# First norm and its modulation cut from two halves of the features into four quarters

## The reference, cut to what matters

```python
mod = c @ w_ada[l] + b_ada[l]                       # c: 1 x 1024, w_ada: 1024 x 3072
shift, scale, gate = jnp.split(mod, 3, axis=-1)
h = _rmsnorm(x, norm_g[l]) * (1.0 + scale[:, None, :]) + shift[:, None, :]
proj = h @ w_in[l]                                  # q_a, k_a, v_a, z_a, ... from h
```

## Time and profile before

| | before |
|---|---|
| median of 3 runs | 1303.47 us |
| the profiled execution's own time | 1301.79 us |
| its span in the trace | 1300.0 us |
| PE busy | 1258.9 us (97%) |
| DVE busy | 757.2 us (58%) |
| ACT busy | 585.0 us (45%) |
| POOL busy | 747.1 us (57%) |
| mean granted clock of TensorE | 0.991 |

### The profile page before, as it was taken

One profiled execution on the slowest core, in us unless ns is written; L12 is line 12 of the kernel. 1 busy time (PEld: TensorE's weight loads), 2 busy tenths in 40 slices (PEclk: granted clock), 3 DMA queues, 4 the chain that ended last, 5 costly groups with the idle time before them and its releaser, 6 DMA issues.

```text
span 1300.0 us, 16886 instructions
## 1 busy us (share of the span) xinstructions
PE 1258.9 (97%) x6162; PEld 1047.0 (81%) x6162; DVE 757.2 (58%) x1233; ACT 585.0 (45%) x951; POOL 747.1 (57%) x862
## 2 busy tenths in 40 slices
PE   5989999999999999999999999999999999999997
PEld 4868878878888888887778988888888888888885
DVE  5857788434434367699687427655457616651564
ACT  3366566456655346233456645434333313331341
POOL 2643543433343676676445869534659857885782
PEclk9989999999999999999999999999999999999998
DMA  9421224232334743232214443222313333223221
GB/s 380 168 82 57 81 81 140 96 98 93 110 115 135 242 128 99 81 98 89 61 69 154 131 163 114 81 66 65 93 55 112 100 112 97 97 98 98 97 81 65
DMA packets 41698, 142.46 MB, mean 110 GB/s; under 512 B 4624, under 2 KB 5136, under 8 KB 40464
## 3 DMA queue, kind: packets, MB, share of 16 engines
q1 hardware_dynamic: 41616, 141.39, 32.7%
HBM read 130.88 MB, written 8.39 MB: 107 GB/s over the span
## 4 chain that ended last, share of the span: by engine, by line
PE 70%; DVE 19%; ACT 6%; issue 2%; POOL 1%; DMA 1%; SPq 0%; DVEq 0%; ACTq 0%; POOLq 0%
PE ps L124 69%; DVE tm L137 4%; DVE ac L137 3%; ACT tm L131 3%; DVE tm L134 2%; ACT L131 1%; PE ps L128 1%; DVE x L137 1%; POOL wl L134 1%; DVE ewl L134 1%; DVE spl L134 1%; ACT wh L131 1%; DVE zh L145 1%; DMA x<-xin 1%; DVE ewh L145 1%
## 5 line engine op out<-in xcount | busy, mean ns | idle before, releaser
L134 POOL TENSOR_TENSOR wl<-raw,wh 128x256 fp32r<-128x256 f32 x804 | 690.7, 890 | 496.6 <-ACT wh L131 488.7
L131 ACT ACTIVATE wh<-raw 128x1024 fp32r<-128x1024 f32 x201 | 212.2, 1056 | 319.3 <-PE ps L124 308.2
L124 PE MATMUL ps<-hh,wh 128*128 128x512 f32 x872 | 344.1, 395 | 0.0
L124 PE MATMUL ps<-hh,wl 128*128 128x512 f32 x872 | 340.5, 391 | 0.0
L124 PE MATMUL ps<-hl,wh 128*128 128x512 f32 x872 | 340.3, 390 | 0.0
L124 PEld LDWEIGHTS ps<-hh,wl 128*128 128x128 f32 x872 | 164.1, 188 | 35.1
L124 PEld LDWEIGHTS ps<-hh,wh 128*128 128x128 f32 x872 | 164.2, 188 | 33.3 <-DVE tm L137 0.4
L124 PEld LDWEIGHTS ps<-hl,wh 128*128 128x128 f32 x872 | 164.3, 188 | 33.0
L134 DVE TENSOR_TENSOR tm<-tm,tm 128x512 f32<-128x512 f32 (+3 forms) x110 | 90.7, 829 | 46.5 <-ACT tm L131 43.6
L137 DVE SCALAR_TENSOR_TENSOR tm<-cb,par_sb,tm 128x512 f32<-128x512 f32 x88 | 87.4, 993 | 50.9 <-ACT tm L131 47.5
L131 ACT ACTIVATE tm<-tm 128x512 f32<-128x512 f32 (+3 forms) x109 | 53.8, 530 | 83.8 <-DVE tm L137 67.8
(11 more groups left out here) (305 smaller groups left out, 2281.4 us busy)
## 6 DMA issues: line engine op xcount, KB each, us to landing
raw<-units SPq DMA_DIRECT2D x201, 512.0 KB, 3.5
ada<-units SPq DMA_DIRECT2D x16, 512.0 KB, 14.6
kept<-ge SPq DMA_DIRECT2D x16, 256.0 KB, 2.8
tm<-kept SPq DMA_DIRECT2D x16, 256.0 KB, 3.7
tm<-gate_w SPq DMA_DIRECT2D x12, 256.0 KB, 3.9
x<-xin SPq DMA_DIRECT2D x2, 1024.0 KB, 6.2
x<-xin SPq DMA_DIRECT2D x1, 2048.0 KB, 10.9
out<-x SPq DMA_DIRECT2D x8, 256.0 KB, 2.2
```

Of the source, the lines that this page charges most:

```text
L124: return self.none if self.e is None else self.e.matmul(out, lhs, rhs, start=start, stop=stop, skip_group_check=skip)
L131: return self.none if self.e is None else self.e.activation(out, in_, func, **kw)
L134: return self.none if self.e is None else self.e.tensor_tensor(out, a, b, op)
```

## The change

A unit of w_ada now holds two row blocks (2k and 2k + 1) of 256 columns of scale and 256 of shift, so four units are a quarter of the features (two blocks of h), and there are 4 quarters of 8 steps of 512 columns in place of 2 halves of 8 steps of 1024. `MQ` names the four quarters of `MA` and `MA2`. The sums, gains and shifts are made by quarter, PE starts a step u of the values when the rows of quarter u are there, DVE puts three steps of the next quarter ahead of a quarter's small instructions, one behind its rows and four behind its low rows, and the loads stand in another order. ACT loads the table of the square root after the fourth square. Renamings that follow from it (`s_mod` keys 2 to 4) are left out here.

```diff
-    u = [("ada", a, k) for a in range(2) for k in range(8)]
+    u = [("ada", a, k) for a in range(4) for k in range(4)]
...
-        def ada_sums(a, b, ma):
...
+        def ada_sums(a, b):
+
+            take(b)
+            pe.wait_ge(s_mod, a, 7)
             for f in range(4):
...
+                last = pe.mm(PS[b][:, f:f + 1], MQ[a][:, f * 128:(f + 1) * 128], con_f("one", 1), True, True)
             last.then_inc(*s_modp.up(a))
             bank[b] = (s_modc, (a,))
...
+        ada_sums(0, 0)
         spread("x", 7)
         bank[7] = (s_ht, ("1", 7))
-        ada_sums(0, 0, MA)
-
-        def second_half(u):
+
+        def next_quarter(u):
 
 
             if u == 2:
                 qkz("a", 0, "q", 0)
-                mod_end(1, 6, MA2)
+            if u:
+                ada_sums(u, 6)
+            if u == 2:
                 qkz("a", 0, "k", 0)
...
-                act.wait_ge(s_mod, 0, j - N_ADA + 2)
+                act.wait_ge(s_mod, 1, 2 * (j - N_ADA - 2) + 1)
...
-        act.wait_ge(l_con, 0)
+            if k == 3:
+                act.wait_ge(l_con, 0)
+                act.fn(sm[:, 60:61], con_raw[:, 0:1], ACT.Sqrt)
...
-        def mod_step(a, k, ma):
-            j = 8 * a + k
+        def mod_step(a, k):
+            j, w = 4 * a + k // 2, slice(512 * (k % 2), 512 * (k % 2) + 512)
...
         for k in range(KC):
-            if k == 6:
-                root_inverse("x")
-            mod_step(0, k, MA)
-        mod_pair(0, 0)
...
+            mod_step(0, k)
+        root_inverse("x")
+        for a in range(4):
+
+            steps = list(range(KC)) if a < 3 else []
+            for k in steps[:3]:
+                mod_step(a + 1, k)
+            mod_pair(a, 6 if a else 0)
+            dve.wait_ge(s_gain, "g", a)
+            dve.wait_ge(s_spread, "x")
+            row(2 * a)
+            row(2 * a + 1)
+            for k in steps[3:4]:
+                mod_step(a + 1, k)
+            low_row(2 * a)
+            low_row(2 * a + 1)
+            for k in steps[4:]:
+                mod_step(a + 1, k)
...
-                pool.wait_ge(s_mod, 0, j - N_ADA + 4)
-                if j == N_ADA + 3:
-                    pool.wait_ge(s_ada, 0)
+                pool.wait_ge(s_mod, 1, 2 * (j - N_ADA) + 1)
...
         for j in range(N_ADA):
+            if j == 12:
+                raw(N_ADA + RING)
             sp.dma(ADA[j][:, :], units[j]).then_inc(*l_ada[j].up("ada"))
-            if j in (5, 7, 11, 13):
-                raw(N_ADA + (5, 7, 11, 13).index(j))
+            if j in (3, 4, 7, 9):
+                raw(N_ADA + (3, 4, 7, 9).index(j))
```

More of the change, by code:

```diff
@@ L324, in build @@
     MA2 = at("ma2", [P, U], F32, a1 + 4096)
+    MQ = [t[:, 512 * x:512 * x + 512] for t in (MA, MA2) for x in range(2)]
     o_ada = [h0, h0 + 4096, h0 + 16384, h0 + 20480] + [w0 + 16384 * x + 4096 * y for x in (1, 2) for y in (2, 3)]
@@ L406, in build @@
     s_add, s_root, s_sqrt, s_spread = sig("s_add"), sig("s_root"), sig("s_sqrt"), sig("s_spread")
-    s_conr, s_mk, s_mod, s_ada, s_modp, s_modc, s_gain = (
-        sig(n) for n in ("s_conr", "s_mk", "s_mod", "s_ada", "s_modp", "s_modc", "s_gain"))
+    s_conr, s_mk, s_mod, s_modp, s_modc, s_gain = (
+        sig(n) for n in ("s_conr", "s_mk", "s_mod", "s_modp", "s_modc", "s_gain"))
     s_ht, s_hh, s_hl = sig("s_ht"), sig("s_hh"), sig("s_hl")
@@ L546, in mod_end @@
             bank[b] = (s_modc, (part,))
-        def ada_sums(a, b, ma):
-            pe.wait_ge(s_mod, a, 6)
+        def ada_sums(a, b):
+            take(b)
+            pe.wait_ge(s_mod, a, 7)
             for f in range(4):
-                pe.mm(PS[b][:, f:f + 1], ma[:, f * 128:(f + 1) * 128], con_f("one", 1), f == 0, False, skip=True)
-            pe.wait_ge(l_ada[8 * a + 7], "ada")
-            for f in range(4):
-                last = pe.mm(PS[b][:, f:f + 1], ADA[8 * a + 7][:, f * 128:(f + 1) * 128], pcol("c", 7), False, True,
-                             skip=True)
-            last.then_inc(*s_ada.up(a))
-            pe.wait_ge(s_mod, a, 7)
-            for f in range(4, 8):
-                last = pe.mm(PS[b][:, f:f + 1], ma[:, f * 128:(f + 1) * 128], con_f("one", 1), False, True, skip=True)
+                last = pe.mm(PS[b][:, f:f + 1], MQ[a][:, f * 128:(f + 1) * 128], con_f("one", 1), True, True)
             last.then_inc(*s_modp.up(a))
@@ L1314, in scalar_program @@
         for k in range(KC):
-            act.wait_ge(s_modc, k // 4)
+            act.wait_ge(s_modc, k // 2)
             act.wait_ge(s_ht, "1", k)
             act.fn(HH[:, k, :], TM[(3 + k) % 7][:, :], ACT.Identity, bias=sm[:, k:k + 1]).then_inc(*s_hh.up("1", k))
-            if k == 2:
+            if k == 1:
                 hi(("aq", 0))
+                hi(("ak", 0))
             if k == 3:
-                hi(("ak", 0))
                 refill(("av", 0))
+            if k == 5:
                 refill(("av", 1))
@@ L1852, in mod_pair @@
             dve.wait_ge(s_gain, "one", a)
-            dve.tt(g, g, prow("norm_g", 4, o), ALU.mult).then_inc(*s_gain.up("g", a))
+            dve.tt(g, g, prow("norm_g", 2, o), ALU.mult).then_inc(*s_gain.up("g", a))
         def mod_out(part, b):
             dve.wait_ge(s_modp, part)
-            dve.tt(sm[:, 8 * part:8 * part + 8], PS[b][:, 0:8], prow("b_ada", 8, 8 * part),
+            dve.tt(sm[:, 16:24], PS[b][:, 0:8], prow("b_ada", 8, 16),
                    ALU.add).then_inc(*s_modc.up(part))
@@ L1878, in vector_program @@
         for k in range(KC):
-            if k == 6:
-                root_inverse("x")
-            mod_step(0, k, MA)
-        mod_pair(0, 0)
-        dve.wait_ge(s_gain, "g", 0)
-        dve.wait_ge(s_spread, "x")
-        row(0)
-        row(1)
-        low_row(0)
-        row(2)
-        low_row(1)
-        mod_step(1, 0, MA2)
-        low_row(2)
-        row(3)
-        mod_step(1, 1, MA2)
-        low_row(3)
-        for k in range(2, KC):
-            mod_step(1, k, MA2)
-        mod_pair(1, 6)
-        dve.wait_ge(s_gain, "g", 1)
-        row(4)
-        row(5)
-        for k in range(4, KC):
-            low_row(k)
-            if k < 6:
-                row(k + 2)
+            mod_step(0, k)
[15 more added lines that the diff above has]
+                mod_step(a + 1, k)
         dve.wait_ge(l_cont, 0)
@@ L2062, in gate_add @@
                 dve.wait_ge(l_gate[x], k)
-                key = (2, k) if x else (2, k, "half")
+                key = (4, k) if x else (4, k, "half")
                 if k == 0:
@@ L2666, in sync_program @@
                     sp.dma(KV[:, p0:p1, :], KVT[:, p0:p1, :]).then_inc(*l_kv[x].up(0))
-            raw(j)
+            if j > N_ADA + RING:
+                raw(j)
         for f in range(KC):
@@ L2702, in pack_units @@
         if k == "ada":
-            r, c0 = slice(128 * u[2], 128 * u[2] + 128), 512 * u[1]
-            b = np.concatenate([wada[r, 1024 + c0:1536 + c0], wada[r, c0:512 + c0]], axis=1)
+            c0, b = 256 * u[1], []
+            for k in (2 * u[2], 2 * u[2] + 1):
+                r = slice(128 * k, 128 * k + 128)
+                b += [wada[r, 1024 + c0:1280 + c0], wada[r, c0:256 + c0]]
+            b = np.concatenate(b, axis=1)
         elif k in ("aq", "ak", "az", "bq", "bk", "bz"):
```

29 lines of the change are left out of this document (14 added, 15 removed).

## The result

The changed kernel takes 1311.62 us in the median of six runs (1309.63 to 1312.53), the kernel before 1302.05 beside it (1301.49 to 1304.37): a ratio of 1.0066, with an interval of 1.0056 to 1.0076. It is slower, by some 7 to 10 us; the forecast was 5.5 over the kernel before. (Two executions further down, one of fill_all and one of quarter_sums2, took 2085 us at a granted clock of 0.56 and stand in no median, range or ratio.)

The account below looks back on a forecast made before the run. PE was taken as the bound from 29.39 us. A head start of 3.5 less 8.2 lost in holes, steps and small instructions gave 4.7 later, with the clock +5.5: 1303.47 + 5.5, about 1309, range 1303.5 to 1313.

Parts of the forecast that it names:

- PE as the bound, one to one: From 29.39 us PE works without a hole, so any shift of its memory sums at 63.03 reaches the end whole.
- Head start 3.4 to 3.5: Up to the first matmul: quarter 0's sums and rows finish sooner, first matmul at about 25.9 in place of 29.39.
- The first hole: Behind quarter 1's sums: PE idle from 35.0 to 37.8 us until quarter 1's rows are made.
- The clock: PE behind the holes: at least one fall to half clock expected behind 37.8 us, 1.6 us more.
- The new wait for the memory norm: At PE's memory sums: the norm's chain ends at 67.9, 2 us behind PE, so 63.03 becomes about 67.8, 4.7 later.
- Costed at nothing: Raw 4's load queued ahead of unit 12, and POOL's units at other times with room of 4 us or more: no cost.
- The faster one: Rival, chance 0.12: DVE never waits for the sums and POOL doesn't slow it, so -3.2 us, 1300.3.
- The slow clock's: Rival, chance 0.10: PE's clock falls in each hole and stays down through a value step, +10 to 12 us, 1314.5.
- The middle of the two cases: Half weight between no clock fall and one of 1.6 us, on top of 4.7 us: +5.5 us.

Follow-up runs that it names:

- fill_all: The changed kernel with q and k cut by quarters, each piece straight behind that quarter's sums on PE: 1302.08 us, ratio 1.0000 to the kernel before.
- quarter_sums2: The kernel before with half 0's sums and rows by quarters, and half 1's sums behind q's half and k's blocks 0 and 1: 1303.87 us, ratio 1.0006.
- shift: The kernel before with a chain of eight 128x512 additions on DVE ahead of the first row, delaying the rest: 1309.07 us, ratio 1.0045.
- early_raw: The kernel before with one transfer reordered, weight unit 28 sent ahead of 26 and 27: 1297.63 us, ratio 0.9957.
- fill: The changed kernel with sums straight behind each value step and q's and k's first halves cut into pieces behind them: 1306.20 us, ratio 1.0012 to the kernel before.
- idle_pool: The changed kernel with three of four POOL subtractions of the first six weight units replaced by zero fills: 1306.21 us, ratio 1.0038 to the kernel before.
- fewer_steps: The changed kernel with every second step of DVE's running sums replaced by a one-column instruction: 1308.37 us, ratio 1.0039 to the kernel before.

## Why the prediction was right, point by point

- **PE as the bound, one to one.** One to one is right: shift moved the end by 5.9 for 6.07. PE as the only bound is not. DVE's running sums were level with it at 45.8 us, and the 0.4 us of idling that the prediction names ahead of the earlier trace rows is PE's weight load waiting for them. In shift whatever PE gained went into waits for DVE. That `sph`'s wait comes of the load at 75.83 was right too, and early_raw shows it.
- **Head start 3.4 to 3.5.** 3.66. The sums started at 12.74 (forecast 12.95), the square root ran at 15.45 without a table load, the rows started at 24.02 (24.3). What released them was not what the prediction had: PE's spread was through at 23.4 (24.1), and DVE's three steps and small instructions, 1.39 us beside POOL, lasted to 24.0. That the number came out so near is luck in part. The steps of 512 columns took 0.81 alone and 1.17 beside POOL (0.82 and 1.15): four in 4.70 at 53.32, two in 1.61 at 44.32. Here the Trainium skill's page "VectorE: DVE Perf Modes", section "The TRN2 errata", from which the prediction estimated 0.16 us for cutting a step in two, does not cover the pairs beside POOL, which cost 0.65 more than one step of 1024 (2 x 1.17 less 1.69).
- **The first hole.** Forecast 35.0 to 37.8, measured 34.00 to 37.60. PE's clock rose after 3.4 us of dense matmuls and not after 5.3, so its sums came a microsecond early, and that was lost at once: DVE had the last step of quarter 1 done at 31.4 as costed, but it did not wait from there: three steps of quarter 2 stand ahead of the small instructions in its program and last to 34.5. They would have been hidden behind sums that end at 35.0.
- **The clock.** This is the mis-sized term. One fall of 1.6 us was expected, at half weight. The first hole brought a stretch from 36.0 to 42.8, of which 5.2 us fell on matmuls (2.4 us lost), and the last a second from 63.3 to 66.7 (1.6). Everything from 45 to 60 us came 1.1 to 1.4 later than forecast: sums of quarter 2 at 48.43 (47.0), rows of quarter 3 at 59.83 (58.7). The two falls took 4.0 us where 0.8 was carried.
- **The new wait for the memory norm.** Right on the chain, wrong on the wait. The splits ended at 68.5 (forecast 67.9), but PE, due at 65.9, came at 69.04, late by the 1.1 carried over, the second fall, 1.6, and 0.4 of wider spacing. So 67.8 and 4.7 became 69.04 and 6.0, and the wait for `mpl` that the prediction named as a sign did not show. In fill, which has no fall, the wait shows (0.62). That 5.5 came so near 6.0 at this point is luck in part: PE lost 3.1 us more than forecast, and the 2.0 that it was to be ahead of the splits took up most of that.
- **Costed at nothing.** The load of raw 4 and POOL's new times did no harm: the DMA share stays at 1.0 to 42.8, and PE never waits for a weight before 75 us.
- **The rivals.** The faster one wanted each quarter's sums through PE within 0.5 us of DVE's seventh step. That held at quarter 1 (sums through at 34.0, DVE's steps at 34.5) and failed at quarter 2, by 3.5 us, and at quarter 3, by 1.2; its other condition, that POOL doesn't slow DVE, failed throughout. Without POOL's reads and with half of the steps (idle_pool, fewer_steps) the mark stayed at 68.57 and 69.29. The slow clock's was half right: a fall behind the two long holes, none for a whole value step. The middle of the two cases gave 5.5 for 6.0.
- **The end of the run.** 1309.0 was forecast and 1311.62 measured: inside the range of 1303.5 to 1313, just outside the forecast's own 1306.5 to 1311.5. Of what it is over the kernel before, 6.0 is shown in both profiles of the changed kernel; the rest is late half clock, which the prediction did not have.

## What to carry to other kernels

Cutting a producer finer starts the consumer sooner, but every cut adds one round trip between the engines, here 2.34 us from sums to first operand, and pays only where the consumer has other work to put there; move that work first. Look also at the engine that the bound takes its operands from: here DVE was level with PE, to 0.06 us, where a look at PE's idle time alone showed no wait. A wait that "absorbs nothing" is worth following to its end: the one here was a transfer queued behind two that weren't ready, and four lines took it away. And judge a few microseconds by the stretches of the trace as well as by the medians, since half-clock stretches elsewhere in the run can be as large as the effect.

## What the runs showed of the hardware

- TensorE's clock fell to its lower level (1.2 of 2.4 GHz) around idle holes of 3.60 us and of 2.34 us, each with eight one-column passes ahead. In fill, where the holes were 1.74, 0.24 and 0.86, it did not fall there. A hole isn't needed: in the kernel before it fell at 48.60 behind the sixteen passes of 45.85, where PE is busy throughout by the profile. In shift, with the same sixteen passes and 0.83 us of idling ahead of them, it did not fall.
- The late stretches at half clock come in nine of the 14 profiles, and only behind three places of the program (times of the kernel before, whose profile has none): sixteen one-column passes at 511.87, PE's hole of 1.68 us at 697.89, and its hole of 1.13 us with eight one-column passes at 724.40. 3.4 us of them cost 1.5 to 1.7.
- The Trainium skill, page "SBUF — State Buffer", section "Who interferes with whom", tells of an exclusive lock on the read and write ports that VectorE and GpSimd share. What it costs here: the chained step of 512 columns takes 1.17 us beside POOL's subtractions in place of 0.81, that of 1024 columns 1.69 in place of 1.39. On average that is 0.3 to 0.4 us a step, less than half of one of POOL's subtractions (eight in 7.72 us at 16.93); whether single steps wait out a whole one, these means don't show. Worst off are the smallest: four instructions on two columns need 1.39 us beside POOL and 0.59 alone.
